# Two feed-forward layers in seven products per quad: order of the splits, of the row sums and of the last tile's blocks

## The reference, cut to what matters

```python
def _swiglu(x, w1, w3, w2):
    return (jax.nn.silu(x @ w1) * (x @ w3)) @ w2
```

## Time and profile before

| what | value |
|---|---|
| median of 3 runs | 3908.89 us (3905.76 to 3913.74) |
| the profiled execution, its own time | 3917.45 us |
| its span in the trace | 3915.7 us |
| TensorE busy | 3405.7 us, 87% of the span, 29922 matmuls |
| VectorE busy | 2579.9 us, 66% |
| ScalarE busy | 1285.5 us, 33% |
| GpSimd busy | 290.9 us, 7% |
| mean granted TensorE clock | 0.949 of full speed |
| `ffn1` in the trace | about 1858 to 2573 us |
| `ffn2` in the trace | about 3158 to 3915 us |

### The profile page before, as it was taken

The page is one execution under the profiler, slowest core; times in us unless marked ns, Lnnn a source line. Parts: engine busy times, 40 slices in busy tenths (PEclk is TensorE's granted clock), DMA queues, the critical chain, the costliest instruction groups (busy, mean ns, idle before and its releaser), DMA issues. The chain is left out here.

```text
span 3915.7 us, 69698 instructions
## 1 busy us (share of the span) xinstructions
PE 3405.7 (87%) x29922; PEld 2714.7 (69%) x29922; DVE 2579.9 (66%) x3593; ACT 1285.5 (33%) x2061; POOL 290.9 (7%) x251
## 2 busy tenths in 40 slices
PE   2999899999747777769999999989977989999996
PEld 1888677887236767637777777767735767777774
DVE  7565455652556555545877777767786587777776
ACT  2211222223534343323422222235465443222222
POOL 0000000000000000000311111020000021111110
PEclk9999999999879999989999999999968999999998
DMA  4233311232652322132111111110000211111111
GB/s 180 100 112 115 128 55 43 79 104 71 237 151 68 79 52 68 47 127 87 59 49 49 50 64 49 38 45 33 18 12 1 68 62 49 49 49 49 49 49 54
DMA packets 150350, 278.55 MB, mean 71 GB/s; under 512 B 9116, under 2 KB 81964, under 8 KB 149788
## 3 DMA queue, kind: packets, MB, share of 16 engines
q1 hardware_dynamic: 134748, 244.53, 19.0%
q10 hardware_dynamic: 15296, 29.57, 2.1%
HBM read 228.15 MB, written 45.65 MB: 70 GB/s over the span
## 5 line engine op out<-in xcount | busy, mean ns | idle before, releaser
L2517 PE MATMUL PS<-ffn_x_high,ring_b_wh 128*128 128x512 f32 x1120 | 438.1, 391 | 5.3 <-DVE ffn_slots_again L248 5.0
L2518 PE MATMUL PS<-ffn_x_low_again,ring_b_wh 128*128 128x512 f32 x1120 | 437.2, 390 | 0.0
L2759 DVE SCALAR_TENSOR_TENSOR xT<-xT,PS 128x1024 f32<-128x1024 f32 (+1 forms) x320 | 368.5, 1163 | 5.1
L248 DVE TENSOR_TENSOR ring_a_wl<-ring_a_raw,ring_a_wh 128x1024 fp32r<-128x1024 f32 x72 | 88.2, 1226 | 340.0 <-ACT ring_a_wh L245 339.8
L2525 PE MATMUL PS<-ffn_hid_high,ffn_down_high 128*128 128x512 f32 x640 | 255.5, 399 | 39.1 <-DVE xT L2759 36.1
L245 ACT ACTIVATE ring_a_wh<-ring_a_raw 128x1024 fp32r<-128x1024 f32 x72 | 76.1, 1058 | 571.0 <-PE PS L282 546.9
L2742 DVE TENSOR_TENSOR xT<-xT,PS 128x512 f32<-128x512 f32 x280 | 188.1, 683 | 105.3 <-PE PS L2519 103.6
L2527 PE MATMUL PS<-ffn_hid_high,ffn_down_raw_again 128*128 128x512 f32 x640 | 250.4, 391 | 0.0
L2526 PE MATMUL PS<-ffn_hid_low,ffn_down_high 128*128 128x512 f32 x640 | 250.0, 391 | 0.0
L2517 PEld LDWEIGHTS PS<-ffn_x_high,ring_b_wh 128*128 128x128 f32 x1120 | 211.5, 189 | 50.7 <-DVE ffn_slots_again L248 5.9
L2518 PEld LDWEIGHTS PS<-ffn_x_low_again,ring_b_wh 128*128 128x128 f32 x1120 | 211.3, 189 | 44.4
(11 more groups left out here) (514 smaller groups left out, 7851.6 us busy)
## 6 DMA issues: line engine op xcount, KB each, us to landing
ffn_down_raw<-in_ffn_down SPq DMA_DIRECT2D x40, 512.0 KB, 3.5
norm_e_t<-in_ada SPq DMA_DIRECT2D x32, 512.0 KB, 3.7
ring_a_raw<-in_in_o SPq DMA_DIRECT2D x32, 512.0 KB, 4.3
ring_b_raw<-in_ffn_up SPq DMA_DIRECT2D x58, 256.0 KB, 4.3
ring_b_wl_again<-in_ffn_up SPq DMA_DIRECT2D x56, 256.0 KB, 4.2
scan_tin<-scan_in SPq DMA_DIRECT2D x9, 1536.0 KB, 8.8
scan_in<-um SPq DMA_DIRECT2D x20, 641.0 KB, 9.8
ring_a_raw<-in_in_e SPq DMA_DIRECT2D x24, 512.0 KB, 3.6
```

The source lines that it names most:

```text
L2517: nc.tensor.matmul(out, wh[:, k, :], xh[:, o, k], start=k == 0, stop=False)
L2518: nc.tensor.matmul(out, wh[:, k, :], xl[:, o, k], start=False, stop=False)
L2759: nc.vector.scalar_tensor_tensor(x, x, ALPHA if q == N_PLAIN else 1.0, out, ALU.mult, ALU.add)\
```

## The change: what it does

1. At i = 4 ScalarE does `cut(n + 4)` before it waits for the gate's sum and takes the SiLU, in every quad.
2. The first quad's blocks move from (0, 0, 1, 2, 2, 1, 2) to (0, 0, 0, 2, 2, 2, 2), the last quad's from (1, 1, 2, 1, 2, 1, 0) to (1, 1, 2, 1, 1, 0, 2).
3. All row sums are made on VectorE: T1, T2 and T4 in one run before the first `plain_gate`, T3 after the split of T1. GpSimd makes none. The splits come in the order of the products that read them, mixed with the first four weight cuts.
4. In the last quad, both down tiles are cut at i = 4 and the first half of the hidden tile is split at i = 5, into the space of the T1 rows. The gate of the second half comes before the two updates of i = 6.
5. The tail waits less: for the first half of the hidden tile only before block 0, for the second before block 8, for the last combine before block 2, and for the updates from block 3 on.

```diff
@@ constants and counters
-            BLOCKS_AFTER[N_PLAIN] = (0, 0, 1, 2, 2, 1, 2)
+            BLOCKS_AFTER[N_PLAIN] = (0, 0, 0, 2, 2, 2, 2)
+            BLOCKS_AFTER[KF - 1] = (1, 1, 2, 1, 1, 0, 2)
...
+            def t_count(o, i):
+                return KH * (T1, T2, T4, T3).index(o) + i + 1
...
                 def hid_at(u, c):
+                    if c == 0 and u == KF - 1:
+                        return xh[:, T1, 0], xl[:, T1, 0]
@@ gpsimd
                         sums(2)
-                        for i in range(KH):
-                            pool.wait_ge(t_made.h, t_made.base + 2 * i + 2)
-                            nc.gpsimd.tensor_tensor(row_source(T4, i), x_row(0, KH + i), row_source(T2, i), ALU.subtract)\
-                                .then_inc(t_pooled.h, 1)
-                        for i in range(KH):
-                            nc.gpsimd.tensor_tensor(row_source(T3, i), x_row(1, KH + i), x_row(1, i), ALU.subtract)\
-                                .then_inc(t_pooled.h, 1)
@@ tensor, the tail
                         pe.wait_ge(down_low.h, down_low.base + KF)
-                        pe.wait_ge(hid_low.h, hid_low.base + gate_count(KF - 1, 1))
-                        pe.wait_ge(updated.h, updated.base + n0)
                         for i in range(2 * KD):
                             c, m = divmod(i, KD)
-                            if i >= 4:
+                            if m == 0:
+                                pe.wait_ge(hid_low.h, hid_low.base + gate_count(KF - 1, c))
+                            if i == 2:
+                                pe.wait_ge(combined.h, combined_at(KF - 1, 7))
+                            elif i >= 3:
                                 pe.wait_ge(updated.h, updated.base + n0 + i - 3)
@@ scalar, the head
-                        for o in (T2, T1):
-                            for i in range(KH):
-                                act.wait_ge(t_made.h, t_made.base + 2 * i + 2)
-                                x_part(o, i, rows_at(o) + i)
-                        plain_silu(0, 1)
+
+                        def row_parts(o):
+                            for i in range(KH):
+                                act.wait_ge(t_made.h, t_made.base + t_count(o, i))
+                                x_part(o, i, rows_at(o) + i)
+
+                        row_parts(T2)
                         cut(number(N_PLAIN, 0))
                         cut(number(N_PLAIN, 1))
-                        for o in (T3, T4):
-                            for i in range(KH):
-                                act.wait_ge(t_pooled.h, t_pooled.base + (KH if o == T3 else 0) + i + 1)
-                                x_part(o, i, rows_at(o) + i)
+                        row_parts(T1)
+                        plain_silu(0, 1)
                         cut(number(N_PLAIN, 2))
+                        row_parts(T3)
                         cut(number(N_PLAIN, 3))
+                        row_parts(T4)
                         plain_silu(1, 1)
@@ scalar, the loop
+                                cut(n + 4)
                                 if i == 4:
                                     act.wait_ge(combined.h, combined_at(q, 5))
                                     nc.scalar.activation(unit(0), unit(0), ACT.Silu).then_inc(silu_done.h, 1)
-                                cut(n + 4)
+                                    if q == KF - 1:
+                                        cut_down(KF - 2)
+                                        cut_down(KF - 1)
...
+                                if i == 5 and q == KF - 1:
+                                    hidden_high(q, 0, 0)
                                 if i == 6:
                                     act.wait_ge(combined.h, combined_at(q, 7))
                                     nc.scalar.activation(unit(1), unit(1), ACT.Silu).then_inc(silu_done.h, 1)
-                                    act.wait_ge(blocks_done.h, blocks_done.base + block_count(q + 1))
-                                    hidden_high(q, 0, 0)
+                                    if q < KF - 1:
+                                        act.wait_ge(blocks_done.h, blocks_done.base + block_count(q + 1))
+                                        hidden_high(q, 0, 0)
...
-                        cut_down(KF - 2)
-                        cut_down(KF - 1)
@@ vector, the head
+                        def row_sums(o, left, right):
+                            for i in range(KH):
+                                if o in (T2, T4):
+                                    dve.wait_ge(t_made.h, t_made.base + t_count(T1 if o == T2 else T2, i))
+                                nc.vector.tensor_tensor(row_source(o, i), left(i), right(i), ALU.subtract).then_inc(t_made.h, 1)
+
+                        def row_rests(o):
+                            for i in range(KH):
+                                x_rest(o, i, rows_at(o) + i)
+
+                        dve.wait_ge(scaled.h, head.at(scaled) + head.count(1, KD - 1))
+                        row_sums(T1, lambda i: x_row(1, i), lambda i: x_row(0, i))
+                        row_sums(T2, lambda i: x_row(1, KH + i), lambda i: row_source(T1, i))
+                        row_sums(T4, lambda i: x_row(0, KH + i), lambda i: row_source(T2, i))
                         plain_gate(0, 0)
-                        for i in range(KH):
-                            dve.wait_ge(scaled.h, head.at(scaled) + head.count(1, KD - 1))
-                            nc.vector.tensor_tensor(row_source(T1, i), x_row(1, i), x_row(0, i), ALU.subtract)\
-                                .then_inc(t_made.h, 1)
-                            dve.wait_ge(t_made.h, t_made.base + 2 * i + 1)
-                            nc.vector.tensor_tensor(row_source(T2, i), x_row(1, KH + i), row_source(T1, i), ALU.subtract)\
-                                .then_inc(t_made.h, 1)
                         plain_gate(1, 0)
-                        for i in range(KH):
-                            dve.wait_ge(t_pooled.h, t_pooled.base + i + 1)
-                            x_rest(T2, i, rows_at(T2) + i)
-                        for i in range(KH):
-                            x_rest(T1, i, rows_at(T1) + i)
-                        plain_gate(0, 1)
+                        dve.wait_ge(t_made.h, t_made.base + t_count(T4, KH - 1))
+                        row_rests(T2)
                         cut(number(N_PLAIN, 0))
                         cut(number(N_PLAIN, 1))
-                        for o in (T3, T4):
-                            for i in range(KH):
-                                x_rest(o, i, rows_at(o) + i)
+                        row_rests(T1)
+                        row_sums(T3, lambda i: x_row(1, KH + i), lambda i: x_row(1, i))
+                        plain_gate(0, 1)
                         cut(number(N_PLAIN, 2))
+                        row_rests(T3)
                         cut(number(N_PLAIN, 3))
+                        row_rests(T4)
                         plain_gate(1, 1)
@@ vector, the loop
                                 elif i == 4:
                                     combine(unit(0), unit(0), q, 4)
+                                    if q == KF - 1:
+                                        cut_down(KF - 2)
+                                        cut_down(KF - 1)
                                 elif i == 5:
                                     combine(unit(2), unit(2), q, 5)
                                     gate(q, 0, unit(0), unit(2), 6)
+                                    if q == KF - 1:
+                                        hidden_low(q, 0, 0)
...
                                 cut(n + 4)
+                                if i == 6 and q == KF - 1:
+                                    gate(q, 1, unit(1), unit(3), 7)
                                 for _ in range(BLOCKS_AFTER[q][i]):
                                     update(q, m)
                                     m += 1
...
                                 if i == 6:
-                                    gate(q, 1, unit(1), unit(3), 7)
-                                    hidden_low(q, 0, 0)
+                                    if q < KF - 1:
+                                        gate(q, 1, unit(1), unit(3), 7)
+                                        hidden_low(q, 0, 0)
                                     hidden_low(q, 1, 1)
-                        cut_down(KF - 2)
-                        cut_down(KF - 1)
```

More of the change, by code:

```diff
@@ L2303, in ffn_stage @@
             down_high, down_low = conv_done, conf_done
-            t_made, t_pooled, biased_rows = cen_done, y_ready, std_done
+            t_made, biased_rows = cen_done, std_done
             plain_in, out_stored = slot_in[1], slot_in[0]
```

4 lines of the change are left out of this document (2 added, 2 removed).

## The result

| what | before | after |
|---|---|---|
| median | 3911.31 us (3905.76 to 3915.11, 4 runs) | 3847.30 us (3845.06 to 3850.34, 4 runs) |
| the profiled execution, its own time | 3917.45 us | 3846.14 us |
| its span | 3915.7 us | 3844.3 us |
| TensorE busy | 3405.7 us, 87% | 3387.5 us, 88% |
| VectorE busy | 2579.9 us, 66% | 2565.3 us, 67% |

The ratio is 0.9838 with a 95% interval of 0.9821 to 0.9855: 63 us (57 to 70) less. The prediction was 3850 us (3841 to 3867).

The account below looks back on a forecast made before the run. TensorE, busy 87%, was taken as the bound, so only its pauses cost time. Terms 35.4 + 2.4 + 6.5 + 4.0 + 4.3 + 6.9 = 59.5 us less, giving 3849.4 from the median 3908.89; forecast 3850 us (3841 to 3867).

Parts of the forecast that it names:

- Part 1: Quads 3 to 19, both feed-forwards: ScalarE's cut ahead of the SiLU removes a 1.04 us pause per quad; 35.4 us.
- 0.3 us to spare: Inner quads: block 7 allowed at 2153.84, needed by TensorE at 2154.16, so the pause is gone with this margin.
- rival (a): Inner quads: margin used up, block 7 still waits, 0.4 to 0.5 us lost a quad; 3865 us, chance 0.14.
- Quad 20: Same wait as the inner quads, in each layer; 1.2 us gained each, 2.4 us together.
- (d): Every quad: SiLU behind the cut and GpSimd's sum comes late, so slower; 0.03 together with (e) and any mishap.
- (f): Inner quads: another, unseen wait ends at the same point, so no gain there; 24 less, 3885 us, chance 0.05.
- (e): TensorE without pauses granted a lower clock; 5% over the inner quads to end slower; 0.03 with (d) and any mishap.
- Part 2: Head and first quad: row sums leave GpSimd, VectorE 4.3 us earlier; gains 6.5 us in `ffn1`, 4.0 in `ffn2`.
- Rival (b): `ffn2`'s first quad eats Part 2, its bias rows moving the pause, and tails give half; 3859 us, chance 0.10.
- Part 3: Last quad and tail: statistics come earlier, as the 6.17 us idle before the tail shrinks; 4.3 us `ffn1`, 6.9 `ffn2`.
- Rival (c): Tails: VectorE, early everywhere, also starts their second half early, so more gain; 3843 us, chance 0.06.
- The prediction's sentence by that rule: Head: under the exclusive lock, GpSimd's next sum falls among the last splits and would cost one operation.

Follow-up runs that it names:

- the second trace of the kernel after: The kernel after, unchanged, run again beside a later version; median 3844.95 us, ratio 0.9843 to the kernel before.
- the kernel with the old tail: The kernel after with points 4 and 5 of the change undone, and the last quad's blocks of point 2; 3860.78 us.
- the 128x256 operation: The kernel after plus one 128x256 VectorE subtraction on unread scratch rows behind product 4's combine in each inner quad; 3847.08 us.
- the cut first alone: The kernel before with only the high part of the down cut moved ahead of the SiLU at product 4; 3870.86 us, ratio 0.9909.

## Why the prediction was right

**Part 1, inner quads: 35.4 us predicted, 36.7 measured.** The mechanism, its place and the absence of a new wait are shown by undoing the exchange and by making it alone. The pause was put at 1.04 us and was 1.08, since the quad without it takes 29.92 and not 29.96 us: 0.227 us for a matmul was rounded up, 132 times. "0.3 us to spare" was 0.25, and rival (a), which lived on it being used up, did not happen, though one half-sized instruction more would have begun it. Quad 20: 2.4 predicted, 2.6 measured. Rivals (d) and (f) fell with the same rows: the cut is at 2089.45, 0.2 us behind product 4. So did (e), the clock: from 1940 to 2440 us TensorE worked without a pause at a granted clock of 1.00.

**Part 2: 6.5 and 4.0 predicted, 6.64 and 3.97 measured, but not for the reason given.** The working laid all of it to the 4.3 us by which VectorE's rows come earlier. Putting the eight sums back costs 3.9 and 3.4 us, of the 3.9 only 2.1 as a pause and the rest as the slow start behind it. In `ffn1`, 1.1 us of the quad are part 1's (undoing it costs 1.08 there), and part of the rest is a slow start that the same pause once brought and once did not. In `ffn2` the head's 4.57 us come with the sums or with the order of the splits, whichever is there. The step that failed is the one that took VectorE's lead as the cause of the head's gain: the new order of the splits gives it too, and the head can use only one of them. So the match of this term is in part luck, and that of `ffn1` too: of its 6.64 us, 0.69 are the head, which took 46.08 us instead of 45.48 in the second trace of the kernel after, 0.09 less than before. Rival (b) had the right place, as `ffn2`'s first quad gave 0.60 us back, but not the size. That the bias rows would start 4.3 us earlier (4.67: 68.70 us behind the first plain matmul before, 64.03 after), that block 2 would pause 8.1 us (8.17) and that a slow start follows came as worked out.

**Part 3: 4.3 and 6.9 predicted, 5.4 and 7.8 measured**, the mis-sized term. VectorE's first tail update was put 4.4 us earlier in the quad; from product 0 of quad 21 it is 28.98 us instead of 33.77, 4.8 earlier, in `ffn1`, and in `ffn2` as well. From there to the statistics I let `ffn1` take its old 12.66 us and it took 12.02; `ffn2` took 10.15, where 10.3 was allowed. In `ffn1`, TensorE's pause before the statistics is 1.69 us (2.5 predicted). The slow start of 1 us that might come behind it did not come there. From the statistics to the next stage `ffn1` took 32.66 us before and 35.22 after, mostly by a slow start behind the next pause, before line 465. That is not the tail's doing as far as the runs show: the kernel with the old tail took 34.28 us there, and one with the new tail (the 128x256 operation) 32.77.

**Sum: 59.5 predicted, 63.2 in the traces, 63 by the ratio.** The terms that were too small are the tails (2.1), the inner quads (1.3) and quad 20 (0.2). Rival (c), 3843 us, named the tails and is the one that came nearest besides the forecast.

## What to carry to other kernels

When an engine works strictly in order, look at which of its instructions waits for something that ends late while the next one is ready and is needed elsewhere: exchanging two such instructions gave two thirds of this change. Judge such a place by the microseconds to spare there, measured by adding a small harmless instruction, and not by the engine's busy share. Parts of a change that shorten the same wait are not additive, so undo them one at a time before giving each its share, and compare by the stretches they touch when other stages vary by more than the effect.

## What the runs showed of the hardware

**VectorE and GpSimd shut each other out.** In `ffn2`'s head of the kernel after:

```profile
3175.70 4.83 POOL L2468 TENSOR_TENSOR ffn_slots<-ring_b_wl_again 128x512 f32<-128x512 f32 x1 [37.27 <-PE PS L2518]
...
3179.27 0.70 DVE L2740 SCALAR_TENSOR_TENSOR xT<-xT,PS 128x512 f32<-128x512 f32 x1
3179.87 1.21 DVE L248 TENSOR_TENSOR ffn_hid_low<-xT,ffn_hid_high 128x512 fp32r<-128x512 f32 x1
...
3183.80 1.38 POOL L2471 TENSOR_TENSOR ffn_slots<-ffn_slots,ring_b_wl_again 128x512 f32<-128x512 f32 x1 [3.27 <-PE PS L2518]
...
3184.13 1.60 DVE L248 TENSOR_TENSOR ffn_slots_again<-ffn_slots,ring_b_wh 128x512 fp32r<-128x512 f32 x1
```

GpSimd's sum, 1.3 us in most other places, is drawn 4.83 us long beside a stream of VectorE subtractions with two operands in SBUF. It ends at 3180.53, 1.26 us after the start of the gate of line 2740, which reads a bank of PS: it seems to have got in there. VectorE's next subtraction, 0.69 us elsewhere, takes 1.21 and ends 0.55 us after GpSimd's end; the one at 3184.13 takes 1.60 and ends at 3185.73, again 0.55 after GpSimd's (3185.18). The exclusive lock of the Trainium skill ("SBUF — State Buffer", section "SBUF: two separate sides"), under which the one that starts first keeps the shared ports for its whole instruction, fits these rows. The prediction's sentence by that rule had one GpSimd operation as the price of the new order; it was 0.5 us of VectorE and 3.5 us of GpSimd at the first sum, and 0.9 us of VectorE at the second.

The same stands in the chain that paced the kernel before. The down cut of the inner quads, drawn 2.06 us long at 2089.81, overlaps GpSimd's sum of 2089.50, which ends at 2090.79; the same form takes 1.22 us where no sum runs beside it:

```profile
3198.88 1.22 DVE L248 TENSOR_TENSOR ffn_down_raw_again<-ffn_down_raw,ffn_down_high 128x1024 fp32r<-128x1024 f32 x1
```

So 0.84 us of VectorE's time right ahead of the critical combine goes with GpSimd's sum, in both kernels (2.06 us in the earlier trace rows too), and it is more than the margin of a quarter of a us. What moving that sum would give, no run shows.

**The slow start varies.** A slow start is a run of matmuls that start 0.43 us apart, where the granted clock is near half (0.51 in the stretch shown for `ffn2`'s first quad), instead of 0.23 us. Behind the same 6.17 us pause of `ffn1`, with the same instructions, there were 6 such intervals in the kernel before, 11 in the one with the old tail and 5 in the one with the cut first alone. Behind the pause of `ffn1` before line 465 (3.4 us between starts in every trace) there was none in the kernel before, 9 in the kernel after and 3 in its second trace. At 0.2 us each that is 0 to 2 us from one trace to another, and a difference of that size between two traces says nothing about the kernels.
